# Copies of x and memory turned on the host, scan gates projected in row form, in a two-block transformer kernel

## The reference, cut to what matters

```python
h = rmsnorm(x, pre_mix_g)                      # x / rms(x) * gain
aq, ak, av, hq, hf_fwd, hf_bwd, hi, hg = split_columns(h @ w_in, IN_SPLITS)
att = axial_gqa_attention(rope(norm(aq)), rope(norm(ak)), av)
f   = lb + (1 - lb) * sigmoid(hf)              # both directions; log f drives the gated scan
rec = rmsnorm(bidirectional_gated_scan(silu(hq), log f_fwd, log f_bwd, hi)) * silu(hg)
x = x + rmsnorm(concat(att, rec) @ w_out)
m = rmsnorm(mem, mem_norm_g)                   # mem: 256 rows of 1024
k, v = split(m @ w_xkv)                        # keys and values of a cross attention
x = x + rmsnorm(cross_attention(rmsnorm(x) @ w_xq, k, v) @ w_xo)
```

## Time and profile before

| what | value |
|---|---|
| median of three runs | 892.42 us (892.14 to 893.91) |
| span of the profiled execution | 891.2 us |
| time of the profiled execution itself | the run that the profile was taken of is not listed by itself; its span lies 1.2 us under the median |
| PE, PEld busy | 879.5 us, 753.7 us |
| DVE, ACT, POOL busy | 648.1 us, 494.0 us, 92.7 us |
| data moved | 152.25 MB |

### The profile page before, as it was taken

How to read it: one execution, slowest core, us unless ns; L and a number is a source line. 1 busy time by engine, 2 the same in 40 slices (tenths; PEclk the granted TensorE clock), 3 DMA queues, 4 the chain that set the end, 5 groups by cost and what they waited for, 6 DMA issues and landing times.

```text
span 891.2 us, 13262 instructions
## 1 busy us (share of the span) xinstructions
PE 879.5 (99%) x5100; PEld 753.7 (85%) x5100; DVE 648.1 (73%) x1024; ACT 494.0 (55%) x880; POOL 92.7 (10%) x123
## 2 busy tenths in 40 slices
PE   8999999999999999999999999999999999999997
PEld 6988897889889888888789887898888888888885
DVE  5789975574879688789856846677787774766774
ACT  5954665464577465566635366676555772324341
POOL 1324100000010000000133300011030100000000
PEclk9999999999999999999999999999999999999999
DMA  9755424453664455556418644344366554564531
GB/s 317 245 168 176 155 95 139 146 201 106 189 212 143 142 181 186 201 188 238 166 60 286 210 142 142 107 166 166 96 232 193 175 180 142 189 212 166 189 142 48
DMA packets 99502, 152.25 MB, mean 171 GB/s; under 512 B 2608, under 2 KB 66352, under 8 KB 99184
## 3 DMA queue, kind: packets, MB, share of 16 engines
q1 hardware_dynamic: 99040, 150.68, 50.6%
q10 hardware_dynamic: 288, 0.47, 0.2%
q0 software_dynamic: 112, 0.26, 0.1%
HBM read 150.35 MB, written 1.05 MB: 170 GB/s over the span
## 4 chain that ended last, share of the span: by engine, by line
PE 90%; DVE 5%; ACT 2%; issue 1%; DMA 1%; POOL 0%; DVEq 0%; POOLq 0%; SPq 0%; ACTq 0%
PE ps L578 27%; PE ps L571 19%; PE ps L1079 13%; PE ps L635 7%; PE ps L1083 7%; PE ps L667 4%; PE ps L742 2%; PE ps L753 1%; DVE sb_wlo L2265 1%; PE ps L830 1%; ACT sb_whi L1630 1%; PE ps L706 1%; PE ps L1027 1%; PE ps L931 1%; PE ps L1223 1%
## 5 line engine op out<-in xcount | busy, mean ns | idle before, releaser
L2265 DVE TENSOR_TENSOR sb_wlo<-sb_ring,sb_whi 128x1024 fp32r<-128x1024 f32 (+2 forms) x169 | 203.6, 1216 | 81.2 <-ACT sb_whi L1630 80.8
L1630 ACT ACTIVATE sb_whi<-sb_ring 128x1024 fp32r<-128x1024 f32 (+2 forms) x169 | 174.0, 1045 | 101.3 <-PE ps L635 70.0
L578 PE MATMUL ps<-sb_whi,sb_tb 128*128 128x512 f32 (+2 forms) x520 | 137.7, 387 | 0.0
L578 PEld LDWEIGHTS ps<-sb_whi,sb_tb 128*128 128x128 f32 x520 | 94.1, 188 | 17.2 <-issue 1.0
L635 PE MATMUL ps<-sb_wlo,sb_tb 128*128 128x512 f32 (+2 forms) x224 | 66.6, 380 | 0.0
L578 PE MATMUL ps<-sb_whi,sb_ta 128*128 128x512 f32 (+1 forms) x240 | 61.4, 380 | 0.0
L1518 POOL TENSOR_SCALAR sb_st<-sb_st 128x1 f32<-128x1 f32 x14 | 7.3, 524 | 451.6 <-ACT sb_probs L1894 451.5
L2223 ACT ACTIVATE sb_b<-sb_b 128x512 f32<-128x512 f32 x9 | 5.7, 632 | 79.7 <-DVE sb_b L2694 79.7
L578 PEld LDWEIGHTS ps<-sb_whi,sb_ta 128*128 128x128 f32 x240 | 42.4, 188 | 8.6 <-issue 0.5
L635 PEld LDWEIGHTS ps<-sb_wlo,sb_tb 128*128 128x128 f32 x224 | 41.5, 188 | 7.8
L2694 DVE TENSOR_REDUCE sb_b<-ps 128x256 f32<-128x512 f32 x36 | 23.9, 686 | 28.6 <-PE ps L1083 28.6
(11 more groups left out here) (430 smaller groups left out, 2065.0 us busy)
## 6 DMA issues: line engine op xcount, KB each, us to landing
sb_ring<-in_w_in SPq DMA_DIRECT2D x32, 1024.0 KB, 5.6
sb_ring<-in_w_up SPq DMA_DIRECT2D x18, 1024.0 KB, 5.1
sb_ring<-in_w_down SPq DMA_DIRECT2D x11, 1024.0 KB, 7.2
sb_ring<-in_w_ffn_down SPq DMA_DIRECT2D x11, 1024.0 KB, 7.5
sb_ring<-in_w_ffn_gate SPq DMA_DIRECT2D x9, 1024.0 KB, 5.3
sb_ring<-in_w_ffn_up SPq DMA_DIRECT2D x9, 1024.0 KB, 5.4
sb_ring<-in_w_xkv SPq DMA_DIRECT2D x8, 1024.0 KB, 5.6
sb_ring<-in_w_out SPq DMA_DIRECT2D x4, 1024.0 KB, 5.0
```

Of the source, the lines that this page charges most:

```text
L578: pe.matmul(o, l, r, start=(start and n == 0), stop=False, skip_group_check=True)
L1630: act.activation(piece_pair(m)[0], src, ACT.Copy).then_inc(s("hi_done"), 1)
L2265: dve.tensor_tensor(low, pieces[m][1], high.bitcast(F32), ALU.subtract).then_inc(s("lo_done"), 1)
```

## The change

- The host passes turned copies of x (with the gain `pre_mix_g` ahead of it) and of mem. The high and low parts of the activations are made straight from them by ACT and DVE, with the gain but without the rows' factor. The 16 transposes of x, the 16 of mem, and the multiplications of the rows' factor into x and mem are gone.
- The first chunk `hff` comes in parts by two queues: ACT issues the two halves of piece 0 and piece 1, SP issues turned x in four parts, then pieces 2 and 3. Its first piece is done by tiles of depth.
- `hff`, `hfb` and `hq` go to row form. ACT applies sigmoid or silu with the rows' factor as scale, and the results are turned afterwards: eight transposes each (`turn_gate`). DVE reads the turned sigmoid from PSUM, ACT copies the turned `hq`.
- The other row-form projections get the rows' factor as they leave PSUM, by the scale of ACT's copy.
- The keys of the cross attention are turned, so their factor differs along the free axis. DVE builds two diagonal matrices, PE multiplies ones by them into one bank (`spread_mem`), ACT copies it out, and DVE multiplies it in as `xkv0` and `xkv1` leave PSUM (`keys_factored`), in the place of ACT's copies.
- Behind each level stand two pieces as before, but each is one place further in the list: `aq` has two pieces ahead of level 0 and not one, and `xkv0` ends ahead of level 8.
- Three matmuls on zeros and not four. The squares of x and mem come later; POOL issues the DMAs of the positions and the row vectors behind the eighth tile of turned x.

The diff, cut to its core. PE:

```diff
-            for cols in (512, 512, 512, 256):
+            for cols in (512, 512, 256):
                 pe.matmul(bank[G[3]][:, 0:cols], probs[:, 0, 0:P], probs[:, 0, 0:cols], start=True, stop=True)
...
-            turned_tiles("pre_mix_g")
-            for half in range(2):
-                cols_half("hff", hT1, half)
-            for half in range(2):
-                cols_half("hfb", hT1, half)
-            turn_norm("mem_norm_g")
-            for half in range(2):
-                cols_half("hq", hT1, half)
+            def turn_gate(name, src, at):
+                for r in range(R):
+                    pe.wait_ge(*banks.empty(f"{name}.{r}"))
+                for m in range(2):
+                    turn(f"{name}T.{m}", src, [2 * m, 2 * m + 1], M[at + m], 1)
+
+            first_piece()
+            gemm_rows("hff", hT1, (1, 4))
+            gemm_rows("hfb", hT1)
+            pe.wait_ge(s("col_in"), 16)
+            turn_gate("hff", hff_rows, 0)
+            gemm_rows("hq", hT1, (0, 2))
+            turn_gate("hfb", hfb_rows, 2)
+            gemm_rows("hq", hT1, (2, 4))
+            gemm_rows("aq", hT1, (0, 1))
+            turn_gate("hq", hq_rows, 0)
+            gemm_rows("aq", hT1, (1, 2))
...
-            after_level(8, (turn_qk1,), (cols_half, "xkv0", memT, 1, (1,)))
+            def spread_mem():
+                banks.take(pe, "mem_factor", M[2])
+                pe.wait_ge(s("mem_diag"), R)
+                pe.matmul(bank[M[2]][:, 0:S], ones, diag, start=True, stop=True).then_inc(banks.fill("mem_factor"), 1)
+            after_level(0, (gemm_rows, "aq", hT1, (2, 4)))
...
+            after_level(5, (gemm_rows, "hg", hT1, (2, 4)), (spread_mem,))
+            after_level(6, (mem_tiles,), (cols_half, "xkv0", memT, 0))
+            after_level(7, (cols_half, "xkv0", memT, 1))
+            after_level(8, (turn_qk1,))
```

SP and POOL:

```diff
+            for q in range(4):
+                part = slice(KT * (q > 0) + 2 * q * S, KT + 2 * (q + 1) * S)
+                sp.dma_start(turned_x[:, part], a["turned_x"][:, part]).then_inc(s(f"turned_x_in{q}"), 16)
+            load_part(FIRST, 2)
+            load_part(FIRST, 3)
+            load_part("hfb", 0)
             for r in range(R):
                 sp.dma_start(x[:, r, :], a["x"][r * P:(r + 1) * P, :]).then_inc(s(f"x_in{r}"), 16)
-            load_all(names[:SLOTS])
+            load_part("hfb", 1)
+            load("hq")
+            sp.dma_start(memT_raw, a["turned_mem"].rearrange("p (k n) -> p k n", n=S)).then_inc(s("turned_mem_in"), 16)
             sp.dma_start(mem, a["mem"].rearrange("(r p) n -> p r n", p=P)).then_inc(s("mem_in"), 16)
...
             step(pool.memset(neghalf[:, :], -0.5))
-            for r in range(R):
-                sums, rstds = (t[:, r:r + 1] for t in stats["pre_mix_g"])
-                rstd("pre_mix_g", [(s("pre_mix_g_sq"), r + 1)], sums, D, rstds)
+            pool.wait_ge(s("first_hi"), KT)
             pool.dma_start(posi[:, :], a["positions_2"].rearrange("(r p) -> p r", p=P),
                           allow_slow_non_contiguous=True).then_inc(s("pos_in"), 16)
```

ACT:

```diff
+            for k in range(2):
+                act.dma_start(raw[FIRST][0][:, k, :], chunks[0][1][0][1][0][1][k * P:(k + 1) * P, :]
+                              ).then_inc(s(f"first_half_in{k}"), 16)
+            dst, w = chunks[0][1][1][1][0]
+            act.dma_start(dst, w.rearrange("(k p) n -> p k n", p=P)).then_inc(raw_sem[FIRST, 1], 16)
...
+                for k in range(KT):
+                    if k < 2:
+                        act.wait_ge(s(f"first_half_in{k}"), 16)
+                        act.activation(high[:, k, :], raw[FIRST][0][:, k, :], ACT.Copy
+                                       ).then_inc(s("hi_done" if k else "first_w_hi"), 1)
+                    if k % 2 == 0:
+                        act.wait_ge(s(f"turned_x_in{k // 2}"), 16)
+                    act.activation(hT1[0][:, k, :], xT[:, k, :], ACT.Copy, scale=first_gain[:, k:k + 1]
+                                   ).then_inc(s("first_hi"), 1)
+                    if k in (3, 5, 7):
+                        ahead_of(FIRST, (k + 1) // 2)
+                    if k == 5:
+                        act.dma_start(ident_col[:, :], a["ident_col"]).then_inc(s("col_in"), 16)
+                        act.dma_start(cst[:, :], a["tables"]).then_inc(s("const_in"), 16)
...
+            ahead_of("hff", 6)
+            for r in range(R):
+                act.wait_ge(s(f"x_in{r}"), 16)
+                act.activation(rows[:, r, :], x[:, r, :], ACT.Square, accum_out=stats["pre_mix_g"][0][:, r:r + 1]
+                               ).then_inc(s("pre_mix_g_sq"), 1)
...
+            def before_mem():
+                ahead_of("hq", 4)
+                spread_keys(1, "fb")
+                ahead_of("hq", 5)
+                gather_keys(1)
+                for r in range(R):
+                    apply("hq", r, hq_rows, ACT.Silu)
...
+            before_mem()
+            act.wait_ge(s("mem_in"), 16)
+            for r in range(R):
+                act.activation(rows[:, r, :], mem[:, r, :], ACT.Square, accum_out=stats["mem_norm_g"][0][:, r:r + 1]
+                               ).then_inc(s("mem_norm_g_sq"), 1)
             ahead_of("hq", 6)
+            for m in range(2):
+                take_rows(f"hqT.{m}", hq[:, m * 512:(m + 1) * 512])
```

DVE (the order in which it comes to the angles, and behind the values of the scan):

```diff
+            for k in range(KT):
...
+                if k in (3, 5, 7):
+                    ahead_of(FIRST, (k + 1) // 2)
             dve.wait_ge(s("col_in"), 16)
...
             dve.wait_ge(s("const_in"), 16)
             dve.tensor_copy(mask_rows[:, :], cst[:, C_QROW:C_QROW + 2 * P]).then_inc(s("mask_ready"), 1)
             dve.wait_ge(s("pos_in"), 16)
...
             dve.tensor_scalar(ang[:, 1], ang[:, 1], 3.1415925, -3.1415925, ALU.min, ALU.max).then_inc(s("angles"), 1)
-            ahead_of("hfb", 1)
+            ahead_of("hfb", 2)
...
                 dve.tensor_tensor(rec[:, r, :], psum(f"rec.{r}"), hgate[:, r, :],
                                   ALU.mult).then_inc(banks.release(f"rec.{r}"), 1)
             ahead(reached["level8"] + 2)
+            def keys_factored(name, at):
+                o, d = (t.rearrange("p (j n) -> p j n", n=S) for t in (psum(name), xkT_flat[:, at:at + 512]))
+                dve.tensor_tensor(d, o, mem_factor.unsqueeze(1).to_broadcast([P, 2, S]), ALU.mult
+                                  ).then_inc(banks.release(name), 1)
+            dve.wait_ge(*banks.empty("mem_factor"))
+            for half in range(2):
+                keys_factored(f"xkv0.{half}", half * 512)
```

More of the change, by code:

```diff
@@ L356, in build @@
         HALF = SLOT // 2
-        T_FORM = ("hff", "hfb", "hq", "xkv0", "xkv1", "w_xq0", "w_xq1")
+        FIRST = "hff"
+        T_FORM = ("xkv0", "xkv1", "w_xq0", "w_xq1")
         slot_at = [0]
@@ L779, in _, with first_piece, both_rows @@
[L779 to L786 removed]
+            def first_piece():
+                high, low = piece_pair(0)
+                piece_at[0] = 1
+                keys = [f"{FIRST}.{r}" for r in range(R)]
+                for key in keys:
+                    banks.take(pe, key, next_g())
+                def both_rows(k, T, w):
+                    for r, key in enumerate(keys):
+                        mm = pe.matmul(bank[banks.at[key][0]][:, :], T[:, k, r * P:(r + 1) * P], w[:, k, :],
+                                       start=k == 0 and T is hT1[0] and w is high, stop=False, skip_group_check=True)
+                    return mm
+                for k in range(2):
+                    pe.wait_ge(*(hi_done(0) if k else (s("first_w_hi"), 1)))
+                    pe.wait_ge(s("first_hi"), k + 1)
+                    both_rows(k, hT1[0], high)
+                    pe.wait_ge(s("first_lo"), k + 1)
+                    both_rows(k, hT1[1], high)
+                    pe.wait_ge(*(lo_done(0) if k else (s("first_w_lo"), 1)))
+                    mm = both_rows(k, hT1[0], low)
+                piece_used(0, mm)
+                for k in range(2, KT):
+                    waits_at[k, None] = [(s("first_lo"), k + 1)]
@@ L799, in level @@
                     for half in range(2):
-                        pe.wait_ge(*banks.empty(f"hq.{half}"))
+                        pe.wait_ge(*banks.empty(f"hqT.{half}"))
                 else:
@@ L1696, in _ @@
-            for half in range(2):
-                ahead_of("hff", 5 + 2 * half)
-                apply(f"hff.{half}", FD[:, half * 512:(half + 1) * 512], ACT.Sigmoid)
-            def forget_hfb():
-                for half in range(2):
-                    ahead_of("hfb", 5 + 2 * half)
-                    apply(f"hfb.{half}", FD[:, NS + half * 512:NS + (half + 1) * 512], ACT.Sigmoid)
-            pre_norm("mem_norm_g", mem, [[(s("mem_in"), 16)]] * R, memT, gain_at("mem_norm_g"), forget_hfb)
+            ahead_of("hff", 8)
@@ new lines, in _, with spread_keys @@
+            ahead_of("hfb", 6)
+            for r in range(R):
+                apply("hfb", r, hfb_rows, ACT.Sigmoid)
+            ahead_of("hfb", 7)
```

(9 more changed lines are left out.)

201 lines of the change are left out of this document (108 added, 93 removed).

## The result

The changed kernel takes 903.06 us (median of 4 runs, 902.58 to 903.26), before 892.52 in the same session: ratio 1.0115, 95% interval 1.0102 to 1.0127. It is slower, 7.8 us over the forecast of 895.3 and 5.1 us over the top of the range. The profiled execution spans 900.8 us against 891.2, so 9.6 us are to be found.

What follows compares the result with a forecast made beforehand. PE bounds the kernel, busy 879.5 of 891.2 us. Terms -4.2 + 2.2 + 0.6 + 2.7 + 1.6 = +2.9 us, added to the median 892.4, gave 895.3 us; range 890.4 to 898.0.

Steps and rivals of the forecast that it cites:

- the one of the positions: Early in hfb, PE waits for a low part that DVE makes only after positions, tables and angles: 3.3 us stall.
- end of hfb against before: Start of the kernel: hfb ends at 32.5 us instead of 36.7, so 4.2 us earlier.
- hfb to level 0: From hfb's end to level 0: 16.5 us of work plus 2.1 of stall against 16.4 before, 2.2 us lost.
- scan, with the spreading of mem's factor: In the scan, the 256-column matmul on the diagonals costs PE 0.6 us; distances between levels stay two pieces.
- bank of xkv1: Ahead of xkv1, PE waits for bank G2, which DVE empties only behind rec and a weight piece: 2.7 us.
- one fall near 20 us: PE's clock falls to half once, behind the 3.3 us stall in hfb: 1.6 us; bounds 0 and 1.6 per stall.
- the sentence on ACT's chain: At the start, ACT alternates weight pieces and x tiles: eighth tile done at 12.7 us, three hff pieces at 18.3.
- ACT's chain ... starts only when DVE has done mem's low parts and forget: Before level 0, ACT's key spreading through silu starts near 9.7 us behind hfb, ends about with PE's first aq piece.
- The squares' 2.1 us: Before level 0, ACT squares mem ahead of the high part of aq's second piece: PE stalls 2.1 us.
- Worse: Rival: clock falls behind two stalls, or first weights land 1.5 us later through 2 KB rows: 897 us, chance 0.16.
- The early landing: Rival: positions and tables land soon, no wait in hfb, which ends at 29.2, no clock fall: 890.4 us, chance 0.20.
- The sign given for it: No PE gap near 20 us would show the early landing right and the forecast wrong.

Runs made afterwards that it cites:

- experiment 1: Changed kernel, but SP's load of the first weight chunk's last two tiles no longer waits for DVE's low part of the pair before: 900.98 us, ratio 1.0093.
- experiment 2: On top of experiment 1, DVE makes the low parts of hfb's first two pieces ahead of its wait for positions and angles: 899.5 us, ratio 1.0071.
- e9_forget_first: Also experiment 9: orders of experiment 8, but DVE does forget before hq's last low part, mem's low parts after aq's second piece: 893.87 us, ratio 1.0014.
- experiment 3: Also e3_keys_before_rec: changed kernel, but DVE multiplies the keys' factor into xkv0 ahead of its work on rec: 898.19 us, ratio 1.0058.
- experiment 4: Changed kernel, but hq's last low part (DVE) goes ahead of the second forget, aq's first piece (ACT) ahead of spreading keys: 903.61 us, ratio 1.0120.
- experiment 7: On top of experiment 1, POOL issues the positions and row vectors at the start, not behind the eighth tile: 900.85 us, one run.
- experiment 11: On top of e9_forget_first, DVE takes aq's third low part ahead of hq's forget products, and six of mem's low parts in idle time: 890.98 us, ratio 0.9980.
- experiment 5: Changed kernel, but DVE makes the low parts of turned mem behind the second forget and what follows it: 899.76 us, ratio 1.0075.
- experiment 6: On top of experiment 5, ACT makes the high part of aq's second piece ahead of the squares of mem: 898.82 us, ratio 1.0062.
- experiment 8: Changed kernel with the reorderings of experiment 1, experiment 2, experiment 3, experiment 4, experiment 5 and experiment 6 together: 892.51 us, ratio 0.9997.
- experiment 10: As e9_forget_first, but ACT spreads the keys ahead of aq's first piece: 894.29 us, ratio 1.0019.

## Why the prediction was wrong

The direction was right, and every wait that it named exists, though the one of the positions is covered in after. It came out at +2.9 us where +9.6 were measured in the profiled execution, by its own steps:

| step | predicted | measured in after |
|---|---|---|
| end of hfb against before | -4.2 | -1.5 |
| hfb to level 0 | +2.2 | +5.0, of it 1.7 clock |
| scan, with the spreading of mem's factor | +0.6 | +1.6 |
| bank of xkv1 | +2.7 | +2.8 |
| clock behind xkv1's gap (predicted: one fall near 20 us) | +1.6 | +1.3 |
| rest | 0 | +0.4 |

**The end of hfb.** What failed is the sentence on ACT's chain: "Then ACT does piece 1 (1.03), two tiles (0.76), piece 2 (1.03, and 0.1 for two DMA issues)" and on to three pieces of hff ending at 18.3. I priced the landings of piece 0 and 1 and took all later ones as covered. I read the order of SP's issues but not what each waits for, though the diff has `load_part(FIRST, 2)` and `load_part(FIRST, 3)` as issues of their own. First products at 6.00 (predicted 5.7) and the eighth tile at 13.4 (12.7) were near. From there the piece of weights was missing until 17.96. The stall that I had put at 3.3 us exists, as experiment 1 shows (2.73), but it was covered by this earlier one. "The load is as full in the new order" was wrong for after: 135 GB/s; in experiment 1 it was right. Hfb in experiment 2 ends at 31.3, 5.4 us ahead of before, which is what the start can be worth.

The wait of SP is not all of this miss. With it gone (experiment 1) hfb is 1.7 us ahead of before, not 4.2: the predicted stall comes up, and behind it the predicted fall of the clock, which had its own 1.6 us in the sum. Put together these two terms say 2.6 ahead; most of the last 0.9 is the low part, ready at 23.3 and not at 22.5, as POOL issued the positions at 14.02 and not at 12.8.

**Hfb to level 0.** I had the work right: without waits it takes 50.82 - 31.70 = 19.1 us (`e9_forget_first`), predicted 19.2. What failed is "ACT's chain ... starts only when DVE has done mem's low parts and forget": I followed who waits for ACT and not what else stands behind those two on DVE. The low part of hq's last piece does, and PE wanted it first. The term was also undersized: eight low parts took 4.58 us, 3.25 when moved to a quieter place (`e9_forget_first`). The squares' 2.1 us were rightly sized (1.90 or 1.91 in experiments 1 to 4 and 7) and covered in after.

**The scan.** The spreading of mem's factor cost PE 0.59 us, as predicted (0.6). What the sum put at nothing are PE's other waits for DVE: 0.30 at 61.85 for the low part of aq's third piece, behind the tables and the products of queries, and 0.59 at 95.06 for the copy of a level (line 2503). The small products for the diagonals are not their cause. They took 1.27 us, not under 0.5, but at 98.30, behind both waits, and the next level (102.26) did not wait. Why DVE was late at 95.06 was not tried.

**The bank.** Right in place, releaser and size (2.7 against 2.76), and shown by taking it away (experiment 3).

**The clock.** Predicted one fall near 20 us; two came, at 48 and at 127 us, and none at 20. For a fall at 48 I had no gap there. The one near 20 came in experiment 1 (0.68 from 24 to 28 us, 1.3 us) behind the gap that it was predicted for; in after that gap is covered. The one at 127 I had among the bounds ("1.6 for each of the three stalls") and gave the case of two falls, with others, 0.16.

**The rivals.** "Worse" was the nearest, but its mechanism (slower landing by 2 KB rows) is not what happened: the queue did not go slower, it stood. The early landing, which was to decide from 4.3 us on, did not come true: positions took 5.8 us to land in after, 5.2 in experiment 1, though the tables landed in 2.8 in after. The sign given for it, no gap of DVE's near 20 us, did come, for another reason: PE was held up earlier, by the weights. A missing gap shows only that something else came last. The Trainium skill (DMA: Bandwidth & Descriptors, "Latency and other measured facts") gives a fixed cost of about 2 us; the rows of this transfer of 1 KB disagree in every kernel here, with a queue at 135 GB/s as well as at 397.

## What to carry to other kernels

When a load gets split into parts of its own, read what each issue in the queue waits for, not only its place: one wait in SP's queue holds back every load behind it, and it can hide the stall that you foresaw. When a step is moved onto an engine, list all that stands behind it on that engine with the time at which each is wanted, and put the step into a stretch where the engine idles. A gap removed upstream is waited for again downstream until the order there is mended too; of these orders only the last (experiment 11) brought a gain over the kernel before.

## What was not expected of the hardware

**The same gap does not always bring a fall of the clock.** The gap ahead of xkv1 is 2.76 or 2.77 us long in seven kernels, with the same work around it. The 16 matmuls behind it (2.08 to 2.18 us at full clock) took 2.14 us in experiment 1 and 3.48 to 3.63 in after and in experiments 4 and 7; in experiments 2, 5 and 6 the clock fell part of the way through (2.81, 2.72, 2.92). Those three cost no less, for the lower clock lasts into the matmuls behind: from xkv1 to the next scores it is 5.91 us in experiment 1 and 7.24 to 7.40 in the six others. Windows 20 to 24 us show it behind the gap at 19 us, first in after, then in `e3_keys_before_rec`, where it is 2.14 us long:

```profile
20.00:24.00 4.00, 2.77 (x12) 1.79 (x11) 3.62 (x19) 1.51 (x2) 0.00 (x0) 1.00 1.02 400
```

```profile
20.00:24.00 4.00, 3.94 (x11) 2.94 (x10) 3.62 (x19) 1.72 (x2) 0.00 (x0) 0.57 1.02 402
```

In the second the clock is at its lower level, and PE, being slow, never meets the wait for ACT at 23.59 us that the first shows (1.16 us). Hfb ends at 35.24 in after and at 35.01 in the second, so this fall cost nothing, since a wait followed. What decides over a fall stays open. Between 0 and 135 us the traces of after and of the experiments have 25 gaps of 1.88 to 3.45 us, and the clock fell behind 15: behind 3 of 9 of 1.88 to 1.91 us, 4 of 6 of 2.03 to 2.22, 8 of 10 of 2.73 to 3.45. It also fell behind one of 1.44 us (experiment 5), and not behind one of 3.06 (`e9_forget_first`). Where no wait followed, a fall cost 1.2 to 1.7 us.

**Operations of DVE and of POOL wait for each other's end.** The low parts of turned mem in after and in `e9_forget_first` (the three numbers are the least, the median and the greatest duration in ns), and one of POOL's products between the first two in after:

```profile
L2484 DVE SCALAR_TENSOR_TENSOR sb_tb<-sb_b,sb_col,sb_tb x8: 473/493/1266, 40.6 to 44.7; 128x256 fp32r<-128x256 f32 x8
```

```profile
L2487 DVE SCALAR_TENSOR_TENSOR sb_tb<-sb_b,sb_col,sb_tb x8: 479/480/480, 48.2 to 51.0; 128x256 fp32r<-128x256 f32 x8
```

```profile
41.65 0.67 POOL L1589 TENSOR_TENSOR sb_b<-sb_b 128x256 f32<-128x256 f32 x1
```

One by one the eight of after take 1.27, 0.83, 0.62, 0.51 and then 0.47 us four times. The first four start at 40.59, 41.78, 42.53 and 43.07, each while a product of POOL runs, and each ends 0.28 or 0.29 us behind that product, which ends at 41.57, 42.32, 42.86 and 43.30. That looks like waiting for the rest of POOL's instruction, not like a rate shared out; what DVE loses depends on how long that one still has to run. Six other kernels (experiments 1 to 4, 7 and 11) have the same four durations to 0.02 us, and experiment 8 has them from the second on. Where POOL is near the end of these products (experiments 5 and 6) only the first of the eight is longer, 0.51, and in experiments 9 and 10, where it has finished them, all take 0.48; POOL's small operations of 128x2 beside them change nothing. POOL seems to wait as well: the first product of its six takes 1.89, 3.02 or 4.16 us in these kernels, steps of 1.13 or 1.14, and DVE's low parts of weights beside it start 1.13 apart (38.32 and 39.45 in after). That each is the other's cause rests on these coincidences; it was not tried by itself, and POOL's times are rough in this profile. The Trainium skill (Advanced Engine Details and Errata, "VectorE Performance Modes") says that VectorE's second port to SBUF is shared with GpSimd, and that GpSimd's instructions and those of VectorE that use both ports can block each other. These rows agree with blocking; which mode the operation runs in no run here shows.
